# Chain steps that are soon due, queued in front of a weight unit's high half

## The reference

```python
def first_block(...):
    h = rmsnorm(x, ln1_g[l])
    proj = h @ w_in[l]
    ...
    oa = dilated_attention(qa, ka, va)
    ob, _ = banded_attention(qb[:, None], kb[:, None], vb[:, None], SWA_WINDOW - 1, sinks[l])
    mix = jax.nn.sigmoid(ga) * (oa @ w_branch_a[l]) + jax.nn.sigmoid(gb) * (ob @ w_branch_b[l])
    x = x + mix @ w_out[l]
    x = x + jnp.square(jax.nn.relu(h2 @ w_up[l])) @ w_down[l]

def second_block(...):
    for l in range(DEPTH_2):
        x = x + 0.5 * _swiglu(_rms_norm(x, ffn1_norm[l]), ffn1_wi[l], ffn1_wo[l])
        c = _split_cols(u @ w_in[l] + b_in[l])
        y_sb = _from_heads(_stick_breaking_attention(...))
        y_ml = _mlstm(...)
        y_mla = _mla(...)
        merged = (g[:, :, 0] * (y_sb @ w_up_sb[l])
                  + g[:, :, 1] * (y_ml @ w_up_ml[l])
                  + g[:, :, 2] * (y_mla @ w_up_mla[l]))
        x = x + merged @ w_out[l]
        x = x + 0.5 * _swiglu(_rms_norm(x, ffn2_norm[l]), ffn2_wi[l], ffn2_wo[l])
```

## Time and profile before

| | |
|---|---|
| time, median of 3 runs | 2367.8 us (2367.73 to 2368.5) |
| profiled execution | 2366.94 us |
| its span, first to last instruction | 2365.1 us |
| granted TensorE clock, mean | 0.999 |
| busy PE / PEld / POOL / DVE / ACT | 99% / 81% / 56% / 49% / 42% |
| idle time of PE ahead of L749 | 20.8 us |
| chain that ended last: share of PE | 97% |

### The profile page before, as it was taken

One profiled execution on the slowest core, in us unless ns is written; L12 is line 12 of the kernel. 1 busy time (PEld: TensorE's weight loads), 2 busy tenths in 40 slices (PEclk: granted clock), 3 DMA queues, 4 the chain that ended last, 5 costly groups with the idle time before them and its releaser, 6 DMA issues.

```text
span 2365.1 us, 29594 instructions
## 1 busy us (share of the span) xinstructions
PE 2341.1 (99%) x11084; PEld 1909.6 (81%) x11084; DVE 1164.3 (49%) x1820; ACT 982.2 (42%) x1561; POOL 1321.9 (56%) x1589
## 2 busy tenths in 40 slices
PE   8999999999999999999999999999999999999999
PEld 8777788888888888777788888888887777888887
DVE  5795475422324432479636733333325796365330
ACT  4556644222223233576534432332336755343321
POOL 5774256655656655457345655555554573466554
PEclk9999999999999999999999999999999999999999
DMA  4322133333333333222122333333332221233333
GB/s 159 103 81 72 40 95 98 96 94 98 97 98 111 97 98 106 68 66 81 55 87 83 98 98 98 91 97 98 98 99 69 71 81 54 81 91 98 97 98 98
DMA packets 60862, 212.88 MB, mean 90 GB/s; under 512 B 6704, under 2 KB 8112, under 8 KB 60720
## 3 DMA queue, kind: packets, MB, share of 16 engines
q1 hardware_dynamic: 60576, 210.86, 30.0%
q10 hardware_dynamic: 144, 0.14, 0.0%
HBM read 208.87 MB, written 2.10 MB: 89 GB/s over the span
## 4 chain that ended last, share of the span: by engine, by line
PE 97%; ACT 1%; DVE 1%; issue 0%; POOL 0%; DMA 0%; SPq 0%; ACTq 0%; DVEq 0%
PE banks L749 96%; POOL t L2070 0%; ACT t L1739 0%; PE banks L1048 0%; PE banks L878 0%; DMA t<-in_w 0%; PE banks L928 0%; PE banks L1105 0%; DVE t L1251 0%; DVE t L1437 0%; ACT L2031 0%; DVE t L1582 0%; ACT t L1973 0%; ACT t L1975 0%; DVE t L1579 0%
## 5 line engine op out<-in xcount | busy, mean ns | idle before, releaser
L749 PE MATMUL banks<-t,t 128*128 128x512 f32 (+6 forms) x10796 | 2317.6, 385 | 20.8 <-ACT t L1759 6.0
L749 PEld LDWEIGHTS banks<-t,t 128*128 128x128 f32 (+2 forms) x10796 | 1877.5, 187 | 438.8 <-issue 53.9
L2070 POOL TENSOR_TENSOR t<-t,t 128x256 fp32r<-128x256 f32 x1544 | 1263.2, 849 | 1010.8 <-ACT t L1739 1002.3
L1739 ACT ACTIVATE t<-t 128x1024 fp32r<-128x1024 f32 x385 | 408.0, 1060 | 1074.7 <-issue 584.9
L1251 DVE TENSOR_TENSOR t<-banks,t 128x512 f32<-128x512 f32 x121 | 83.0, 687 | 160.2 <-PE banks L749 158.0
L1418 DVE TENSOR_TENSOR t<-banks,t 128x512 f32<-128x512 f32 x44 | 30.4, 691 | 184.1 <-PE banks L749 184.0
L1386 DVE SCALAR_TENSOR_TENSOR t<-banks,t 128x512 f32<-128x512 f32 x32 | 22.1, 692 | 155.4 <-PE banks L749 155.4
L1134 DVE SCALAR_TENSOR_TENSOR t<-t,t,t 128x512 fp32r<-128x512 f32 x64 | 52.4, 822 | 58.6 <-ACT t L1759 58.4
L1363 DVE TENSOR_TENSOR t<-t,t 128x512 fp32r<-128x512 f32 x68 | 70.0, 1030 | 2.3
L1759 ACT ACTIVATE t<-t,t 128x512 fp32r<-128x512 f32 x64 | 45.5, 715 | 56.7 <-DVE t L1386 49.1
L1392 DVE TENSOR_TENSOR t<-banks,t 128x512 f32<-128x512 f32 x24 | 16.6, 691 | 106.0 <-PE banks L749 106.0
(11 more groups left out here) (190 smaller groups left out, 1260.0 us busy)
## 6 DMA issues: line engine op xcount, KB each, us to landing
t<-in_w SPq DMA_DIRECT2D x386, 512.0 KB, 3.6
t<-in_xT SPq DMA_DIRECT2D x8, 256.0 KB, 6.8
out<-t SPq DMA_DIRECT2D x8, 256.0 KB, 4.6
t<-in_vbias SPq DMA_DIRECT2D x2, 384.0 KB, 3.8
t<-in_c SPq DMA_DIRECT2D x1, 576.0 KB, 8.9
t<-in_w SPq DMA_DIRECT2D x2, 256.0 KB, 4.0
t<-in_pos SPq DMA_DIRECT2D x2, 256.0 KB, 4.4
t<-in_dmask SPq DMA_DIRECT2D x4, 128.0 KB, 4.5
```

The source lines that it names most:

```text
L749: return pe.matmul(o, l, r, start=start, stop=stop, skip_group_check=True)
L1739: a.activation(whl[u % 2][:, 0:1024], wraw[u % 3][:, :], ACT.Copy).then_inc(*w_high.next(u))
L2070: p.tensor_tensor(hl[:, 1024:2048][:, c], wraw[u % 3][:, c], as_f32(hl[:, c]), ALU.subtract).then_inc(*w_low.next((u, q)))
```

## The change

`pump` gets an argument, a time by which a step may be due early. In `prepare`, between the load and the `whalf` of each unit, `pump(AHEAD)` is called with 0.8 us. A step whose first engines hold TensorE ("t") isn't let in early; for every other step the limit is `now() + 0.8`. All other calls of `pump` are as before.

```diff
@@ def prepare(self, u):
         while self.split <= min(u + 1, self.units - 1):
             self.load(self.split + 2)
+            self.pump(AHEAD)
             self.halve()
         self.load(u + 4)
@@
-    def pump(self):
+    def pump(self, ahead=0.0):
 
         moved = True
         while moved:
             moved = False
             self.fill()
             for i in sorted((i for i, g in enumerate(self.slots) if g), key=lambda i: self.slots[i][2]):
-                while self.slots[i] and self.at(self.slots[i][1]) <= self.now():
+                while self.slots[i] and self.at(self.slots[i][1]) <= self.now() + (0.0 if "t" in self.slots[i][1][0] else ahead):
                     self.advance(i)
                     moved = True
@@
 BACKLOG = 0.8
+AHEAD = 0.8
```

## The result

The changed kernel takes 2391.65 us in the median of five runs (2388.6 to 2394.08). The kernel before takes 2367.73 us in runs on the same chip. The ratio is 1.0102, with a 95% interval of 1.0091 to 1.0113: the change makes the kernel 24 us slower. The forecast was 2365.9 us with a range of 2361.0 to 2373.5.

The account below looks back on a forecast made before the run. TensorE, busy in 99% of the span, was taken as the bound, with only its idle time to win. Terms -3.1 + 1.2 = -1.9 us gave 2365.0 for the profiled execution, 2365.9 us as median; range 2361.0 to 2373.5.

Parts of the forecast that it names:

- TensorE has no room and only its idle time counts: Whole span: TensorE 99% busy at full clock; only 13.3 us idle in the stretches with chains can be won.
- (b): Rival: long step ahead of a half makes TensorE wait 2.7 us in each of two layers, 2373.2 us; chance 0.20.
- `sb_logs`: Stick-breaking logarithms on ScalarE start before the high half, free of cost; 1.54 us drain wait gone twice, -3.1 us.
- `low_squares`: Squaring instructions on GpSimd go ahead of the low quarters, which come 0.6 us late, twice: +1.2 us.
- (d): Rival: shared SBUF port lengthens quarters behind `low_squares` and `ml_e`, 4.4 us on top, 2370.3 us; chance 0.05.
- `ml_e`: Last head's exponentials on ScalarE go ahead of a high half; first quarter still 0.6 us in time: 0 us.
- The evacuation of the finished group (L1251): VectorE, behind early chain steps: wanted only a unit (5.44 us) later, takes 0.68 us, so costs nothing.
- Only the steps that pass a half or an evacuation cost: Unstated assumption in the chain stretches: only steps moved in front were priced, their followers given no term.
- Block 1, 0 us: 100 to 300 us: waits for a Newton step and for quarters taken as unchanged, 0, bounds -1.2 and +1.2.
- Feed-forward unchanged: Feed-forward stretches, where no slot holds a chain: unchanged to 0.1 us.
- (a): Rival: nothing won, since the planner moves TensorE's steps earlier too; 2367.8 us, or 2369.0 with the GpSimd term; chance 0.22.
- (c): Rival: freed chains remove two thirds of 10.6 us of waits in their stretches, 2360.8 us; chance 0.13.

Follow-up runs that it names:

- e8: Changed kernel, but only in the mixers and only steps overdue by 1.5 us go ahead of a half, nothing early: 2367.01 us, ratio 0.9997.
- e2: Kernel before, halves untouched, only the evacuation of a projection group put behind a pump with 0.8 us look-ahead: 2388.06 us, ratio 1.0087.
- e1: Changed kernel with the evacuation put directly behind its group's last matmul, ahead of the early pump: 2382.3 us, ratio 1.0064.
- e13: Changed kernel with both halves and evacuations put back ahead of the early pump, look-ahead kept: 2380.94 us, ratio 1.0057.
- e10: Changed kernel with the look-ahead withheld from every step whose engines name VectorE: 2389.82 us, ratio 1.0091.
- e11: Changed kernel with the look-ahead withheld from every step whose engines name ScalarE: 2378.4 us, ratio 1.0045.
- e4: Changed kernel with the early pump called only for units below 100, so in block 1 alone: 2369.12 us, ratio 1.0005.
- e5: Changed kernel with the high half queued ahead of the early pump, look-ahead kept; steps still pass evacuations: 2375.58 us, ratio 1.0036.
- e12: Changed kernel with the look-ahead at 1.6 us instead of 0.8 us: 2409.15 us, ratio 1.0179.
- e6: Changed kernel with the long VectorE step at each mixer's start (`values2`) kept out of the look-ahead: 2389.38 us, ratio 1.0090.
- e9: Changed kernel with the early pump left out at four boundaries, the start of each mixer pair and of its key groups: 2385.57 us, ratio 1.0075.
- e14: Changed kernel with the first tap of the short convolution withheld from the look-ahead: 2394.78 us, ratio 1.0116.
- e15: Changed kernel with `low_rs`, the norm of the low-rank projections, withheld from the look-ahead: 2391.91 us, ratio 1.0107.
- e16: Changed kernel with the edits of e6 and e15 together: 2384.2 us, ratio 1.0077.

## Why the prediction was wrong, point by point

- **TensorE has no room and only its idle time counts.** Right for what could be won. Wrong for what could be lost: the working priced a wait at its length. Here 13.8 us of new idle time came with 7.9 us (second trace: 10.6 us) of longer busy time, about 5 to 8.5 us of it by the clock. No wait past the start-up in the earlier trace rows is over 1.5 us, so the trace of before showed no price for a longer one; rival (b) named a wait of 2.7 us and should have carried this as its upper end.
- **`sb_logs`, -3.1 us.** The mechanism came true. In the changed kernel the logarithms start at 946.75 and the high half at 950.51, the reverse of the earlier trace rows, and the wait for L1940 is gone in both layers. The gain did not arrive. In e8, which has it without the losses, the gain is 0.5 us with an interval that holds zero. The step "So their price is nothing" was wrong: with the logarithms of the widest part in front of a half, its quarters come 0.84 and 0.85 us late. That is the mechanism of rival (b) at a third of its 2.7 us.
- **`low_squares`, +1.2 us.** It came true in kind, with the forecast at half the size: the row at 1043.60 shows 1.25 us for L2072 behind them, and layer 1 the same, so 2.5 us in place of twice 0.6. Eight quarters behind the squares ran from 1042.37 for 8.01 us, 1.0 us each against the 739 ns in the median of the earlier trace rows; that is the direction of rival (d), by 0.26 us a quarter and not 1.4. Over the span the waits for the quarters still grew by 0.5 us only (4.7 to 5.2), since the two of 0.97 us ahead of the key groups are no longer there.
- **`ml_e`, 0 us.** Right: the rest of a mixer pair, behind the key groups, loses 0.6 and 0.4 us.
- **"The evacuation of the finished group (L1251) is now behind such steps on VectorE. Two banks take turns, so it is wanted only a unit (5.44 us) later, and it takes 0.68 us: nothing."** This is the step that failed. The cover was taken from a quiet stretch of projections and used for the whole kernel. At the key groups a group lasts 0.69 us, and at the wide group that opens a mixer pair banks just freed are wanted at once. There the cover is under 1 us, against up to 3 or 4 us of chain steps. And the 0.68 us is the length of the evacuation, where what had to be priced was the length of all that can stand ahead of it. The waits for L1253 sum to 14.5 us, where the prediction had nothing. e2, which does only this, loses 20.6 us, and e1, which undoes only this, takes away 9.9 of the 14.4 us of new idle time in the mixers.
- **Only the steps that pass a half or an evacuation cost.** This was in the working without being said: each part was "moved in front", and the steps behind it in its chain were taken as unmoved. e13 passes nothing at a boundary and still loses 13.8 us, 9.7 us of it in the mixers with 4.1 us of new idle time; e10 and e11 show that the early ScalarE steps bring most of the loss, though it is VectorE that TensorE waits for. The prediction named this in its last sentence as a way to be wrong ("waits stand at lines which have none now") and gave it 0.02.
- **Block 1, 0 us, bounds ±1.2.** The waits did move within the bounds: the two for L1273 are one of 2.28 us now, and the 1.20 us of the earlier trace rows is gone. With the clock the lag is 1.1 to 3.7 us in the traces; by the runs of e4 it is 1.7 us, with an interval that holds zero. What the prediction left out is that these waits hang on the order too: with the halves first (e5) all three are gone.
- **Feed-forward unchanged.** Right, to 0.00 us.
- **The rivals.** (b) asked for a sum of waits for L2070 over 8 us; it is 5.2 us, and 10.2 us only in e12. Late halves were not the main mechanism in the changed kernel. (a) fell with the wait for L1940, (c) with the time, and (d), 2370.3 us, is 21 us short. None of the four had the evacuation in it.

**What stays open.** No single step was found whose place decides. e6, e9, e14, e15 and e16 withhold the suspects one by one and give back 2, 6, 0, 0 and 6 us of the 24 (e14 and e15 are 27.6 and 25.7 us over before). In e14 the same three taps stay in front of the evacuation, in e15 `low_rs` takes their place, and e6 touches the start of the pair alone. What is shown: the two places, that VectorE's line is what TensorE waits for there, that late evacuations alone bring such a loss (e2) and that putting them back takes away most of the new idle time in the mixers (e1), the growth with the look-ahead, and the part of the clock. That the order of VectorE's line as a whole is the cause, and not one member, is argued from what is left when the members are taken out; it was not shown by a run that puts the whole of the old VectorE order under the new ScalarE order.

## What to carry to other kernels

Before a step is hoisted in a planned order, look at everything that is put into the same engine's line later and is wanted soonest, and price the hoisted steps, with their own waits and their followers, against that one's cover. Take the cover from the place with the shortest groups, not from a quiet stretch. And price a new wait of TensorE of some 2 us above its length, since the matmuls behind it may run at half clock (here up to 3.4 us more for one place, where 6.8 us ran at 1.2 GHz). Where a total mixes stages, compare the stages: here block 1 hid the order of the experiments.

## What the runs showed of the hardware

In these traces TensorE's granted clock fell to 1.2 GHz behind waits of 1.5 to 2.9 us in an otherwise full line, sometimes and not always for the same wait in the same program: behind the 2.53 us at a pair's start it fell in layer 1 in the first trace (1765 to 1775 us) and in neither layer in the second. The same instruction stream took 2386.8 and 2389.6 us of span with waits that are equal to 0.1 us past the start-up. In the kernel before it fell once past the start-up, in the second trace, behind the waits of 1.47 and 0.40 us for L1273 in block 1, and not in the first:

```profile
178.00:188.00 10.00, 8.44 (x50) 5.84 (x51) 9.83 (x13) 3.78 (x6) 6.84 (x6) 0.83 0.36 106
```

Behind its two waits of 1.54 us for L1940 it did not fall in either trace. That kernel, with no wait over 1.6 us past the start-up, came out at 2365.1 and 2365.3 us.
